# A two-layer transformer kernel on one Trainium2 core: attention heads issued in pairs, and the forget bias as one rounded product

## What is computed

```python
# first block: causal softmax over one block of 256 (the "moba" mixer with one block)   heads 0 to 7
# first block: sliding window of 128, 8 query heads on 2 key/value heads, with a sink    heads 8 to 15
p = jnp.exp(sc - m[..., None])
denom = jnp.sum(p, axis=-1) + jnp.exp(sink - m)
# second block: forgetting attention                                                     heads 16 to 23
F = jnp.cumsum(log_f, axis=-1)
logits = einsum(qs, k) * scale + Fq[..., :, None] - F[..., None, :]   # then causal softmax
# second block: stick breaking                                                           heads 24 to 31
log_beta = log_sigmoid(z); log_one_minus = where(mask, log_sigmoid(-z), 0)
suffix = cumsum(log_one_minus, reverse=True) - log_one_minus
A = where(mask, exp(log_beta + suffix), 0)
```

## Time and profile before

| | |
|---|---|
| Median of 3 runs | 814.56 us (812.58 to 815.51) |
| The profiled execution | 817.81 us |
| its span | 816.0 us |
| TensorE busy | 772.2 us (95%) |
| VectorE, ScalarE, GpSimd busy | 356.1, 308.9, 261.5 us |
| Mean granted TensorE clock | 0.974 |
| HBM read | 201.11 MB, 248 GB/s over the span |

### The profile page before, as it was taken

How to read it: one execution, slowest core, us unless ns; L and a number is a source line. 1 busy time by engine, 2 the same in 40 slices (tenths; PEclk the granted TensorE clock), 3 DMA queues, 4 the chain that set the end, 5 groups by cost and what they waited for, 6 DMA issues and landing times.

```text
span 816.0 us, 10583 instructions
## 1 busy us (share of the span) xinstructions
PE 772.2 (95%) x4182; PEld 534.2 (65%) x4182; DVE 356.1 (44%) x648; ACT 308.9 (38%) x535; POOL 261.5 (32%) x103
## 2 busy tenths in 40 slices
PE   4999999999999897999999999899999999999994
PEld 3899987766677675888876767676644344434541
DVE  5232724345628766333233346656332342234225
ACT  5544334445465464443344666431111021201113
POOL 0766626443538456275233336430000000000000
PEclk9999999999999999999999999997899999999998
DMA  9964576253455448555222223339999999999941
GB/s 361 414 235 150 222 275 267 104 206 116 194 186 227 137 165 317 207 198 214 104 104 104 103 104 129 120 145 425 421 432 424 422 394 430 421 430 429 379 171 52
DMA packets 19577, 202.73 MB, mean 248 GB/s; under 512 B 2384, under 2 KB 3152, under 8 KB 7504
## 3 DMA queue, kind: packets, MB, share of 16 engines
q1 hardware_dynamic: 18816, 200.47, 61.9%
q10 hardware_dynamic: 720, 1.70, 0.6%
HBM read 201.11 MB, written 1.05 MB: 248 GB/s over the span
## 4 chain that ended last, share of the span: by engine, by line
PE 83%; DVE 7%; ACT 4%; issue 3%; POOL 2%; DMA 1%; ACTq 0%; DVEq 0%
PE psum L775 14%; PE psum L1075 14%; PE psum L776 13%; PE psum L777 13%; PE psum L1107 7%; PE psum L1048 4%; PE psum L948 3%; PE psum L868 2%; PE psum L1027 2%; PE psum L988 2%; POOL ring_rounded L1387 2%; PE psum L970 1%; ACT ring_rounded L1291 1%; DVE ring_rounded L1585 1%; PE psum L953 1%
## 5 line engine op out<-in xcount | busy, mean ns | idle before, releaser
L1387 POOL TENSOR_TENSOR ring_rounded<-ring,ring_rounded 128x1024 fp32r<-128x1024 f32 (+1 forms) x99 | 261.3, 2662 | 276.1 <-ACT ring_rounded L1291 276.1
L1291 ACT ACTIVATE ring_rounded<-ring 128x1024 fp32r<-128x1024 f32 (+1 forms) x136 | 133.7, 1035 | 20.1 <-PE psum L777 19.0
L775 PE MATMUL psum<-hT_rounded,ring_rounded 128*128 128x256 f32 x360 | 104.8, 291 | 3.7 <-POOL ring_rounded L1387 3.7
L776 PE MATMUL psum<-work_rounded,ring_rounded 128*128 128x256 f32 x360 | 103.2, 287 | 0.0
L777 PE MATMUL psum<-hT_rounded,ring_rounded 128*128 128x256 f32 x360 | 103.0, 286 | 0.0
L1585 DVE TENSOR_TENSOR ring_rounded<-ring,ring_rounded 128x1024 fp32r<-128x1024 f32 (+1 forms) x37 | 76.2, 2063 | 43.0 <-ACT ring_rounded L1291 43.0
L775 PE MATMUL psum<-ring_rounded,hT_rounded 128*128 128x512 f32 (+1 forms) x224 | 89.7, 400 | 1.4 <-DVE work_rounded L1490 1.4
L777 PE MATMUL psum<-ring_rounded,work_rounded 128*128 128x512 f32 (+1 forms) x224 | 86.1, 385 | 0.0
L776 PE MATMUL psum<-ring_rounded,hT_rounded 128*128 128x512 f32 (+1 forms) x224 | 86.1, 384 | 0.0
L1075 PE MATMUL psum<-ring,work 128*64 128x512 f32 x320 | 84.7, 594 | 0.0
L775 PEld LDWEIGHTS psum<-hT_rounded,ring_rounded 128*128 128x128 f32 x360 | 70.3, 195 | 8.4 <-POOL ring_rounded L1387 4.5
(11 more groups left out here) (240 smaller groups left out, 1158.1 us busy)
## 6 DMA issues: line engine op xcount, KB each, us to landing
ring<-in_chunks SPq DMA_DIRECT2D x44, 2048.0 KB, 8.1
ring<-in_expert_w_down SPq DMA_DIRECT2D x16, 2048.0 KB, 13.2
ring<-in_expert_w_gate SPq DMA_DIRECT2D x12, 2048.0 KB, 13.9
ring<-in_expert_w_up SPq DMA_DIRECT2D x8, 2048.0 KB, 16.8
gates<-in_expert_w_up SPq DMA_DIRECT2D x4, 2048.0 KB, 23.6
hT<-in_expert_w_gate SPq DMA_DIRECT2D x4, 1024.0 KB, 15.1
mixed<-in_expert_w_gate SPq DMA_DIRECT2D x4, 1024.0 KB, 17.1
ring<-in_chunks SPq DMA_DIRECT2D x4, 512.0 KB, 8.9
```

Source lines behind the costliest of these rows:

```text
L775: nc.tensor.matmul(out, a[0], b[0], start=start, stop=False, skip_group_check=True)
L776: nc.tensor.matmul(out, a[0], b[1], start=False, stop=False, skip_group_check=True)
L1291: nc.scalar.activation(as_rounded(high(c)[:, piece]), src[:, piece], ACT.Copy).then_inc(chunk_hi, 1)
L1387: nc.gpsimd.tensor_tensor(as_rounded(w[:, piece]), w[:, piece], was_rounded(high(c)[:, piece]), ALU.subtract)\
```

## The change

- Steps are laid out by pairs of heads: S of pair p+1, T of pair p and a new step P of pair p+1 in one turn, V of pair p in the next. P holds what VectorE and ScalarE do for a pair's probabilities; S is TensorE's alone. The number of turns is the same, 18 in each block.
- `scores` issues even and odd head alternately, in the two row halves; `values` alternately in the two column halves. Sliding-window heads are paired across the key/value groups, so the host packs columns of bz, rows of w_proj_b and the sinks accordingly.
- The forget bias is one product of 384 columns per head in fp32r, in front of the scores. F is split on VectorE into a rounded high part and a rounded rest, at partitions 0 and 32 and again at 64 and 96 (`fox_split`), 40 rows of which each half reads; the weights are a broadcast column of `fox_pick`, -1 in the two rows of the head.
- On VectorE, masks of both heads come first, then maxima of both, then what follows exp.
- `o_done` and `scores_done` count pairs.

```diff
+    def pairs_of_heads(first):
+        turns = [[("S", first), ("P", first)], []]
+        for p in range(first, first + 8):
+            more = p + 1 < first + 8
+            turns.append([("S", p + 1)] * more + [("T", p)] + [("P", p + 1)] * more)
+            turns.append([("V", p)])
+        return turns
...
-    todo = list(range(0, 18))
+    todo = pairs_of_heads(0)
...
-        if n == 10:
+        if n == 11:
             steps.append(("y_split", "c"))
             low_due = "c"
-        if n == 11:
+        if n == 12:
             steps.append(("y_split", "a"))
             low_due = "a"
...
+            def scores(p):
+                wait_operands(p)
+                if p:
+                    pe.wait_ge(scores_masked, 2 * p)
+                pair = [(score_bank[h % 2],) + operands(h)[0:2] for h in (2 * p, 2 * p + 1)]
+                if p < 12:
+                    fox_pair = 8 <= p
+                    if fox_pair:
+                        for h in (2 * p, 2 * p + 1):
+                            rows = slice(HD * (h % 2), HD * (h % 2) + 40)
+                            nc.tensor.matmul(score_bank[h % 2][:, 0:384],
+                                             as_rounded(fox_pick[rows, h - 16:h - 15]).to_broadcast([40, P]),
+                                             as_rounded(fox_split[rows]), start=True, stop=False, skip_group_check=True)
                     for t, (lo, n) in enumerate(((0, P), (P, T))):
-                        last = nc.tensor.matmul(b[:, lo:lo + n], q[:, t * P:(t + 1) * P], k[:, 0:n],
-                                                start=True, stop=not fox_head)
-                        if fox_head:
-                            row = fox_neg_ident[:, h - 16:h - 15].to_broadcast([8, P])
-                            last = nc.tensor.matmul(b[:, lo:lo + n], row, fox[:, 2, 0:n], start=False, stop=True)
+                        for b, q, k in pair:
+                            last = nc.tensor.matmul(b[:, lo:lo + n], q[:, t * P:(t + 1) * P], k[:, 0:n],
+                                                    start=not fox_pair, stop=True, skip_group_check=True)
                 else:
-                    nc.tensor.matmul(b[:, 0:T], k[:, 0:P], q[:, 0:T], start=True, stop=True)
-                    last = nc.tensor.matmul(b[:, T:T + P], k[:, P:T], q[:, P:T], start=True, stop=True)
+                    for b, q, k in pair:
+                        nc.tensor.matmul(b[:, 0:T], k[:, 0:P], q[:, 0:T], start=True, stop=True)
+                    for b, q, k in pair:
+                        last = nc.tensor.matmul(b[:, T:T + P], k[:, P:T], q[:, P:T], start=True, stop=True)
                 last.then_inc(scores_done, 1)
...
+                pe.wait_ge(pt_evicted, 2 * p + 2)
+                pair = [(h % 2, o_bank[HD * (h % 2):HD * (h % 2) + HD, :], operands(h)[2]) for h in (2 * p, 2 * p + 1)]
+                for at, o, v in pair:
+                    nc.tensor.matmul(o[:, 0:T], v[0], probT[:, at, 0:T], start=True, stop=False,
                                      skip_group_check=True)
+                for at, o, v in pair:
+                    last = nc.tensor.matmul(o[:, P:T], v[1], probT[:, at, T:T + P], start=False, stop=True,
                                             skip_group_check=True)
+                last.then_inc(o_done, 1)
...
-            v.tensor_scalar(fox_neg_ident[:, :], ident[0:8, 0:8], -1.0, None, ALU.mult)
+            picked = hstat[0:104, 0, 0:8]
+            link(v.tensor_reduce(picked, ident[0:104, :].rearrange("p (b j) -> p j b", b=4)[:, 0:8, :], X, ALU.add))
+            v.tensor_scalar(as_rounded(fox_pick[:, :]), picked, -1.0, None, ALU.mult)
...
+            def probs(p):
+                dve.wait_ge(scores_done, p + 1)
...
+                for h in pair:
+                    masked(h)
+                for h in pair:
...
+                        ins = v.tensor_reduce(st[:, 0:1], s[:, 0:P], X, ALU.max, negate=True)
+                        ins = v.tensor_reduce(st[:, 1:2], s[:, P:384], X, ALU.max, negate=True)
...
+                for h in pair:
+                    dve.wait_ge(exp_done, h + 1)
...
                  .then_inc(fox_ready, 1)
+                zeros = cs("mask_causal")[0:104, P:T].unsqueeze(1).to_broadcast([104, 3, P])
+                link(v.tensor_copy(as_rounded(fox_split).rearrange("p (a b) -> p a b", a=3), zeros))
+                dve.wait_ge(fox_ready, 1)
+                high_at, low_at = fox_split[0:8], fox_split[32:40]
+                v.tensor_copy(as_rounded(high_at[:, 0:P]), fox[:, 2, 0:P])
+                link(v.tensor_copy(as_rounded(high_at[:, P:384]), fox[:, 2, :]))
+                v.tensor_tensor(as_rounded(low_at[:, 0:P]), fox[:, 2, 0:P], was_rounded(high_at[:, 0:P]), ALU.subtract)
+                link(v.tensor_tensor(as_rounded(low_at[:, P:384]), fox[:, 2, :], was_rounded(high_at[:, P:384]), ALU.subtract))
+                v.tensor_copy(as_rounded(fox_split[HD:HD + 8]), was_rounded(high_at))
+                v.tensor_copy(as_rounded(fox_split[HD + 32:HD + 40]), was_rounded(low_at)).then_inc(fox_split_done, 1)
```

More of the change, by code:

```diff
@@ L118, in heads @@
         for _ in range(n):
-            h = todo.pop(0)
-            for kind, g in (("S", h), ("T", h - 1), ("V", h - 2)):
-                if first <= g < last:
-                    steps.append((kind, g))
+            steps.extend(todo.pop(0))
+    def pairs_of_heads(first):
[5 more added lines that the diff above has]
+        return turns
     ada = list(range(2 * N_MOD))
@@ L159, in plan @@
     steps.append(("load_final_g", 0))
-    first, last = 0, 16
-    todo = list(range(0, 18))
+    todo = pairs_of_heads(0)
     seq = [(("fm", "bq", 0), 1), (("fm", "bq", 1), 1), (("bkv",), 1), (("mix", 0), 0), (("mix", 1), 0)]
@@ L228, in plan @@
     unit("FT",)
-    first, last = 16, 32
-    todo = list(range(16, 34))
+    todo = pairs_of_heads(8)
     seq = [(("fm", "qb", 1), 1), (("fm", "kb", 0), 1), (("fm", "kb", 1), 2), (("tm", "h0", 0), 1),
@@ L922, in operands @@
                 if h < 16:
-                    g = (h - 8) // 4
-                    lo = HD * g
-                    return (qs[lo:lo + HD, (h - 8) % 4], kvs[lo:lo + HD, 0:T],
-                            [kvs[:, T + t * P + g * HD:T + t * P + (g + 1) * HD] for t in range(TT)])
+                    lo = HD * (h % 2)
+                    return (qs[lo:lo + HD, (h - 8) // 2], kvs[lo:lo + HD, 0:T],
+                            [kvs[:, T + t * P + lo:T + t * P + lo + HD] for t in range(TT)])
                 i = h % 8
@@ L958, in scores, with turn @@
                 last.then_inc(scores_done, 1)
-            def turn(h):
-                b = trans_bank[h % 2]
-                if h >= 2:
-                    pe.wait_ge(pt_evicted, h - 1)
-                pe.wait_ge(probs_ready, h + 1)
-                if h < 24:
-                    for j in range(3):
-                        last = nc.tensor.transpose(b[:, j * P:(j + 1) * P], score[:, h % 2, j * P:(j + 1) * P], ident)
-                else:
-                    nc.tensor.matmul(b[:, 0:384], cs("suffix"), soft[:, h % 2, :], start=True, stop=False,
+            def turn(p):
+                for h in (2 * p, 2 * p + 1):
+                    b = trans_bank[h % 2]
+                    if p:
+                        pe.wait_ge(pt_evicted, h - 1)
+                    pe.wait_ge(probs_ready, h + 1)
+                    if p < 12:
+                        for j in range(3):
+                            last = nc.tensor.transpose(b[:, j * P:(j + 1) * P], score[:, h % 2, j * P:(j + 1) * P], ident)
+                    else:
+                        nc.tensor.matmul(b[:, 0:384], cs("suffix"), soft[:, h % 2, :], start=True, stop=False,
+                                         skip_group_check=True)
+                        last = nc.tensor.matmul(b[:, P:T], ones[:, 0:P], soft[:, h % 2, T:T + P], start=False, stop=True,
+                                                skip_group_check=True)
+                    last.then_inc(pt_done, 1)
@@ new lines, in turned, with outputs @@
+            def turned(p):
+                for h in (2 * p, 2 * p + 1):
+                    if h >= 24:
+                        dve.wait_ge(pt_done, h + 1)
+                        s = score[:, h % 2, :]
+                        v.tensor_tensor(s, s, trans_bank[h % 2][:, 0:384], ALU.subtract).then_inc(stick_ready, 1)
+            def outputs(p):
+                dve.wait_ge(o_done, p + 1)
+                mixer = (0, 1, 0, 1)[p // 4]
+                y = mixed[:, mixer, p % 4, :]
+                if p < 8:
+                    if p in (0, 4):
+                        dve.wait_ge(*evicted(("fm", "cz" if p == 0 else "bz", 1)))
@@ L1756, in _ @@
                     n += 1
-                elif s[0] not in ("begin", "split", "y_split", "sigmoid", "load_final_g"):
```

(6 more changed lines are left out.)

126 lines of the change are left out of this document (49 added, 77 removed).

## The result

| | before | changed |
|---|---|---|
| Median, same chip | 814.57 us (4 runs, 812.58 to 815.51) | 786.37 us (4 runs, 785.51 to 789.08) |
| Ratio, 95% interval | | 0.9663 [0.9633, 0.9692] |
| Profiled execution, its span | 817.81, 816.0 | 789.08, 787.1 |
| Mean granted clock | 0.974 | 0.964 |

What follows compares the result with a forecast made beforehand. TensorE, busy 95% of 816.0 us, was taken as the bound. Head work of 85.2 less 55.4 saves 29.8 us; minus 2 us of waits, 27.8 off the 814.56 median gives 786.8, range 779 to 797.

Steps and rivals of the forecast that it cites:

- Score pair: Two heads' score products in the row halves: 1.29 us with weight loads one behind another; bounds 1.06 and 1.49.
- Value pair: Two heads' value products in the column halves: 1.01 us with load and tail, against 1.58 for two heads.
- A second beside B first 0.21: Value products of heads A and B: A's second 256-column record runs beside B's first, 0.21 us, after A's first alone.
- Rival 3: A pair costs what a head did, 0.85 for scores and 0.79 for values; 10.4 us more off, 776; chance 0.04.
- Forget pair: Pair of forget heads: f32 bias products on 8 rows replaced by two rounded ones at 0.25 us; 3.35 us, four times.
- Stick pair: Pair of stick heads, with two products per head where the transposes were: 4.30 us, four times 17.2.
- The products' sum: TensorE's work for all heads falls from 85.2 to 55.4 us, saving 29.8: forget 14.1, plain 10.6, stick 5.1.
- New waits: TensorE waiting for pairs' probabilities ahead of transposes: 3 us new, less 1 us of present waits, 2 us net.
- Rival 2: Pair's softmax late by 1 to 2.5 us at six to eight of sixteen turns; 790 to 796; chance 0.13.
- VectorE at logf: Seven operations behind the scan before the first forget scores, some 2.5 us, costed at nothing; upper end 1 to 2 us wait.
- Expert loop: TensorE-bound loop behind the attention; its loads come earlier with TensorE's steps, so it keeps its length, costed at nothing.
- Sizes by stretch: Attention stretches of the old trace: 100 to 262 us 10 to 11 us shorter, 385 to 505 us some 17.

Runs made afterwards that it cites:

- the first experiment: Changed kernel with the probabilities step of pair 1 moved behind the two mix units instead of ahead of the modulation units; 773.53 us, ratio 0.9499.

## Why the forecast came out, point by point

- **Score pair, 1.29 forecast, 0.85 measured.** The failed step is "eight loads at 0.11 come one behind another if loads don't overlap". Loads of the two row halves do overlap, with each other and with products (eight loads in 0.52 us; in one row half, 1.17): a pair adds nothing to a head, below even the lower bound of 1.06. The error is 16 x 0.44 = 7.0 us. "TensorEngine Tiling (Array Packing)" of the Trainium skill, Key Properties, states that different tiles can load weights and multiply in parallel; 0.85 against 1.50 in one half agrees, and I had set another page's rule, on the price of a single load, beside the row instead.
- **Value pair, 1.01 forecast, 0.80 measured.** The failed step is "Records start in order", and with it "A second beside B first 0.21". B's first does not wait for A's second: both halves start together (two records at 401.69), even where the program has them one after the other. 16 x 0.21 = 3.4 us. Rival 3's prices were right, and its chance of 0.04 far too small: I let one arithmetic of beginnings and ends speak against it, and no row.
- **Forget pair, 3.35 forecast.** By rows 0.27 + 0.75 + 0.63 + 0.80 and two entries of 0.09 to 0.10: 2.64. Of the 0.71 less, 0.65 is the two terms above. Bias products side by side, 0.27 for my 0.25: right. Stick pair 4.30 forecast, 3.6 by rows.
- **The products' sum.** Stretch 1 without the wait (145.6, from the first experiment) is 15.7 below before, stretch 2 26.05: 41.7. Of this 2.5 are the three waits of the earlier trace rows that went, and stretch 1 has a new one of 1.0 for a weight piece; so the products saved 40.2 in place of 29.8. The two terms above, 7.0 and 3.4, are that difference.
- **New waits, 2 us net forecast; 11.7 came at one place.** With it came 1.0 for the weight piece and 1.9 more at the second `mT` (why that wait grew no run isolates), and the 2.5 of old waits went. The failed step is the search for lateness only where transposes wait for probabilities. There it was right, and none is seen. What I left out is who else stands behind the pair's probabilities in VectorE's queue: the eviction of the unit ahead of the mix units. The stretching was in my text ("a 0.56 us operation of VectorE takes 2.62"), as a cause for the wrong waiter. Rival 2 had the size (6 to 12 us), but another place: one wait, not six to eight.
- **VectorE at logf: right.** Seven operations, 2.4 us (380.79 to 383.15), no wait at the first forget pair (387.14); FT still waits 1.4 for the scan, as before (1.3). GpSimd's subtract had ended at 380.31, so the upper end, beside GpSimd, was not met. That the scan is itself long by GpSimd is not shown: it takes 2.75 in every run, always begun beside a subtract.
- **Expert loop: right.** From its first product (L1060 at 545.10, before L1048 at 573.82) to the end it is 242.0 us, and 242.2 before. Second `mT` to the end, 298.6, is 295.3 in the first experiment, which has the same 4.0 us wait: it differs by half clock (32.8 and 18.7 us of these stretches), not by the loop.
- **Sizes by stretch: wrong both ways.** "10 to 11 us shorter" was 4.0, "some 17" was 26.05. The time alone would have hidden this.

## What to carry to other kernels

In this kernel, work that filled one half of the array took its neighbour in the other half along for nothing: count such a pair as one, and look for it first. When steps are regrouped, list for each engine not only the consumer of the moved step but every step queued behind it, and look which other engine's instructions run beside it: here four small scalings took 9 us. Such a wait has two remedies. Moving the disturbed step did at least as well where nobody was near to wait for it (pair 1: stretch 1 is 145.6 us, with GpSimd held back 148.4); where another eviction stood close behind, at `mT`, it only passed the wait on, and holding back the engine that disturbs gained 9.6 us.

## What was not expected of the hardware

- VectorE's scalings, and its operations with two inputs from SBUF, mostly take 1.9 to 2.9 us beside GpSimd's 128x1024 subtracts instead of 0.29 to 0.69, about as long as one subtract (2.4 us when alone). Size does not matter: one on 128x8 (L1617) takes 2.38 there (263.21) and 0.16 elsewhere (480.97). tensor_reduce (0.28, 0.41), the reciprocal (0.15), the masks from PSUM (0.5) and ScalarE's scaling (0.39, 0.49) are not touched. "SBUF — State Buffer" of the Trainium skill, Who interferes with whom, describes it: VectorE's copies and scalings with two ports, and operations with two SBUF inputs, block behind a GpSimd instruction for its whole length, tensor_reduce and operations with one SBUF input outside those modes don't. All these rows agree.
- Row halves overlap wholly in float32, weight loads included, and without alternation: 0.85 to 0.87 us a pair against 1.50 in one half. Column halves do so too: 0.80 against 1.44.
- TensorE's granted clock was at 1.2 GHz for 10.2 us around the wait of 9.25 us and for 6.8 us around that of 4.0 (491.5 to 498.3), part of it in the work behind them. This makes a wait dearer than it shows: 9.25 us cost 11.7.
